# A two-layer hybrid encoder trunk on one core: the probability-times-value products of both attentions with high and low parts side by side in one matmul

## What is computed

```python
def hybrid_layer(x, w_in, a_group_w, a_scale, b_sinks, c_rel_bias, w_out, ln_gain, ln_bias):
    h = jnp.einsum('bsd,de->bse', x, w_in)
    a_v, a_gate, b_q, b_k, b_v, b_gate, c_q, c_k, c_v, c_gate = jnp.split(h, _split_points(), axis=-1)
    a_out = pool_mixer(a_v, a_group_w, a_scale) * jax.nn.silu(a_gate)
    b_out = swa_sink_attention(b_q, b_k, b_v, b_sinks) * jax.nn.silu(b_gate)
    c_out = chunk_relbias_attention(c_q, c_k, c_v, c_rel_bias) * jax.nn.silu(c_gate)
    mix = jnp.concatenate([a_out, b_out, c_out], axis=-1)
    y = jnp.einsum('bse,ed->bsd', mix, w_out)
    return _layer_norm(DEEPNORM_ALPHA * x + y, ln_gain, ln_bias)
# in both attentions
    p = jax.nn.softmax(s, axis=-1)            # B: with a sink column beside the keys
    o = jnp.einsum('bnhgqk,bnkhd->bnqhgd', p.astype(vb.dtype), vb)
```

## Time and profile before

| | us |
|---|---|
| median of 3 runs | 2956.86 (2956.52 to 2957.44) |
| the profiled execution, whole | 2955.86 |
| its span in the trace | 2954.1 |
| its mean granted TensorE clock | 0.998 |

### The profile page before, as it was taken

How to read it: one execution, slowest core, us unless ns; L and a number is a source line. 1 busy time by engine, 2 the same in 40 slices (tenths; PEclk the granted TensorE clock), 3 DMA queues, 4 the chain that set the end, 5 groups by cost and what they waited for, 6 DMA issues and landing times.

```text
span 2954.1 us, 46399 instructions
## 1 busy us (share of the span) xinstructions
PE 2923.3 (99%) x14272; PEld 2452.7 (83%) x14272; DVE 1408.8 (48%) x2546; ACT 1196.9 (41%) x2539; POOL 1252.6 (42%) x926
## 2 busy tenths in 40 slices
PE   8999999999999999999999999999999999999998
PEld 7888888888888888888888888888888888888886
DVE  5444555422666655531155555553126666555324
ACT  4443454422444445542244444553224444454421
POOL 4444444444344434444444444443443444344442
PEclk9999999999999999999999999999999999999999
DMA  6343332454344422335554442224553444233342
GB/s 195 118 122 119 87 83 76 131 174 161 117 143 139 138 82 76 83 115 156 151 165 143 146 146 86 80 81 135 168 172 95 146 139 138 79 82 82 125 150 107
DMA packets 189147, 364.13 MB, mean 123 GB/s; under 512 B 18913, under 2 KB 27137, under 8 KB 185345
## 3 DMA queue, kind: packets, MB, share of 16 engines
q1 hardware_dynamic: 185264, 347.25, 38.7%
q10 hardware_dynamic: 3792, 15.73, 1.3%
HBM read 320.94 MB, written 45.11 MB: 124 GB/s over the span
## 4 chain that ended last, share of the span: by engine, by line
PE 95%; issue 3%; DVE 2%; ACT 0%; POOL 0%; ACTq 0%; DVEq 0%; POOLq 0%
PE acc L523 64%; PE sc L523 17%; PE pv L523 11%; PE sc L583 2%; PE sc L629 1%; ACT mixl L861 0%; DVE nmax L1289 0%; DVE sc L1287 0%; PE acc L553 0%; PE pv L547 0%; PE sc L547 0%; DVE mixl L1248 0%; POOL wl L1206 0%; DVE prob L1296 0%; PE sc L559 0%
## 5 line engine op out<-in xcount | busy, mean ns | idle before, releaser
L1206 POOL TENSOR_TENSOR wl<-raw,wh 128x512 fp32r<-128x512 f32 x920 | 1251.9, 1366 | 1657.9 <-ACT wh L861 1621.1
L523 PE MATMUL acc<-xh,wh 128*128 128x512 f32 x2624 | 1037.8, 396 | 11.1 <-DVE xl L1237 7.9
L523 PE MATMUL acc<-xh,wl 128*128 128x512 f32 x2624 | 1024.5, 390 | 0.0
L523 PE MATMUL acc<-xl,wh 128*128 128x512 f32 x2624 | 1023.6, 390 | 0.0
L861 ACT ACTIVATE wh<-raw 128x512 fp32r<-128x512 f32 x920 | 569.1, 629 | 981.3 <-PE acc L523 608.4
L523 PEld LDWEIGHTS acc<-xh,wh 128*128 128x128 f32 x2624 | 493.7, 188 | 109.8 <-issue 10.0
L523 PEld LDWEIGHTS acc<-xh,wl 128*128 128x128 f32 x2624 | 493.1, 188 | 106.0
L523 PEld LDWEIGHTS acc<-xl,wh 128*128 128x128 f32 x2624 | 494.1, 188 | 95.3
L523 PE MATMUL sc<-wh,mixh 128*128 128x512 f32 x496 | 193.4, 390 | 0.1
L523 PE MATMUL sc<-wh,mixl 128*128 128x512 f32 x496 | 193.1, 389 | 0.0
L523 PE MATMUL sc<-wl,mixh 128*128 128x512 f32 x496 | 192.9, 389 | 0.0
(11 more groups left out here) (188 smaller groups left out, 3742.1 us busy)
## 6 DMA issues: line engine op xcount, KB each, us to landing
raw<-in_wall SPq DMA_DIRECT2D x920, 256.0 KB, 2.7
res_scratch<-res ACTq DMA_DIRECT2D x12, 1024.0 KB, 3.9
res<-res_scratch SPq DMA_DIRECT2D x12, 1024.0 KB, 5.0
res<-in_x SPq DMA_DIRECT2D x8, 1024.0 KB, 5.4
x_scratch<-res SPq DMA_DIRECT2D x8, 1024.0 KB, 4.7
prob<-x_scratch SPq DMA_DIRECT2D x32, 256.0 KB, 3.3
res<-x_scratch SPq DMA_DIRECT2D x8, 1024.0 KB, 5.2
hist_scratch<-mixh SPq DMA_DIRECT2D x8, 768.0 KB, 4.5
```

Source lines behind the costliest of these rows:

```text
L523: return nc.tensor.matmul(o, lhsT, rhs, start=start, stop=stop)
L1206: nc.gpsimd.tensor_tensor(wl[:, s, :], raw[:, s, :], wh[:, s, :].bitcast(F32), ALU.subtract).then_inc(w_lo, 1)
```

## The change

**C.** The values are now stored per head: `cv[h]` has the head's high part in 64 columns and its low part in the other 64, as `bv` has them. `pt` holds high and low probabilities side by side (`pt[:, block, head, part, query]`). `c_attend` runs, for each head and block, one matmul of 256 columns (128 queries, high and low): two matmuls for a block in place of three. The result of a group has four parts, one of which (low by low) was not computed before. ScalarE copies the lower 64 rows out (`c_low_rows`, between the two exponentials of the next group), VectorE adds them and then the two halves of the columns (`c_add`), into `c_att`. Each group has a bank of its own (the third takes the first one's again, the fourth one of `sc[0]`). `attention_product` becomes one operation.

**B.** `b_attend` takes both parts of a chunk in one matmul of 256 columns. A tile now fills two double banks, `pv` and `sc[g]`; ScalarE makes four copies in place of two, VectorE four adds of 64x512 and four of 64x256 in place of four of 64x256. `b_fold` counts twice for a tile.

**Order.** PE runs the first quarter of units 20 and 22 ahead of the transposes of groups 1 and 2. A's product goes behind the normalising of group 3. The tanh of a gate goes to the gate's own buffer. ScalarE's splits in the output projection stand one or two places earlier against the input's copies and the store of `res`.

```diff
-        pth = sb("pth", [P, 5, 2, P], F32R)
-        ptl = sb("ptl", [P, 5, 2, P], F32R)
+        pt = sb("pt", [P, 5, 2, 2, P], F32R)
+        pth, ptl = (pt[:, :, :, n, :] for n in range(2))
...
-        cv_h, cv_l = (m[:, MIX_B + 2:MIX_B + 4, :].rearrange("p a (b n) -> p (a b) n", n=P) for m in (mixh, mixl))
+        cv = [m[:, MIX_B + 2:MIX_B + 4, :].rearrange("p a (b n) -> p (a b) n", n=P) for m in (mixh, mixl)]
...
+        c_out = [pv[:, 0:512], pv[:, 512:1024], pv[:, 0:512], sc[0][:, 0:512]]
+        b_out = [[pv, sc[0]], [pv, sc[1]]]
...
             def c_attend(it, p, j):
-                if j == 0:
-                    pe.wait_ge(prod_ok, p * 2 + (MIXES * it + 2))
+                if j < 3:
+                    pe.wait_ge(c_fold, p * 4 + (4 * C_PAIRS * it + j + 1))
                 pe.wait_ge(ct_lo, p * 8 + (8 * C_PAIRS * it + 2 * j + 2 + 2))
                 v0 = 0 if half(it) else 4 - j
-                for v in range(v0, 5):
-                    *_, last = attend(outputs(j), (cv_h, cv_l), j + v, v, slice(0, P), v == v0, v == 4)
+                for h in range(2):
+                    for v in range(v0, 5):
+                        last = mm(c_out[j][:, 2 * P * h:2 * P * (h + 1)], cv[h][:, j + v, :],
+                                  pt[:, v, h, :, :].rearrange("p l q -> p (l q)"), v == v0, v == 4)
...
             def b_scores(it, v, g):
+                pe.wait_ge(b_fold, v * 2 + (2 * B_TILES * it + 1))
...
             def b_attend(it, v, g):
-                pe.wait_ge(b_fold, v + (B_TILES * it + 1))
+                pe.wait_ge(b_fold, v * 2 + (2 * B_TILES * it + 2))
                 for u in range(2):
                     pe.wait_ge(bt_lo, v * 2 + (2 * B_TILES * it + u + 1 + 4))
                     for c in range(4):
-                        n = 4 * u + c
-                        o = pv[:, P * n:P * (n + 1)]
-                        mm(o, bv[:, n, g, :], b_pth[:, u, c, :], True, False)
-                        last = mm(o, bv[:, n, g, :], b_ptl[:, u, c, :], False, True)
-                last.then_inc(b_pv, 1)
+                        last = mm(b_out[g][u][:, 2 * P * c:2 * P * (c + 1)], bv[:, 4 * u + c, g, :],
+                                  b_pt[:, u, c, :, :].rearrange("p l k -> p (l k)"), True, True)
+                    last.then_inc(b_pv, 1)
...
                     quarter(19, 0)
+                    quarter(20, 1, part=range(0, 1))
                     c_transpose(it, p, 1)
-                    quarter(20, 1)
+                    quarter(20, 1, part=range(1, 4))
...
                     nc.scalar.activation(prob[:, h, c0:C_KEYS], sc[h][:, at:at + C_KEYS - c0], ACT.Exp,
                                          bias=nmax[:, h, 0:1], accum_out=psums[:, h, 0:1]).then_inc(cs_exp, 1)
+                    if h == 0 and j:
+                        c_low_rows(it, p, j - 1)
...
+            def c_low_rows(it, p, j):
+                act.wait_ge(c_pv, p * 4 + (4 * C_PAIRS * it + j + 1))
+                act.wait_ge(c_fold, p * 4 + (4 * C_PAIRS * it + j + 1))
+                copy(c_low[ROWS[j % 2], :], c_out[j][HD:P, :]).then_inc(c_low_ok, 1)
...
+            def b_low_rows(it, v, g):
                 for u in range(2):
-                    last = copy(b_low[u], b_out[HD:P, 4 * u:4 * u + 4, :, :])
-                last.then_inc(b_low_ok, 1)
+                    act.wait_ge(b_pv, v * 2 + (2 * B_TILES * it + u + 1))
+                    act.wait_ge(b_fold, v * 2 + (2 * B_TILES * it + u + 2))
+                    for n, rows in enumerate(ROWS):
+                        last = copy(b_low(v, u)[rows, :], b_out[g][u][HD:P, 512 * n:512 * (n + 1)])
+                    last.then_inc(b_low_ok, 1)
...
+            def c_add(it, p, j):
+                dv.wait_ge(c_low_ok, p * 4 + (4 * C_PAIRS * it + j + 1))
+                low = c_low[ROWS[j % 2], :]
+                V_(V.tensor_tensor(low, c_out[j][0:HD, :], low, ALU.add))
+                sums_ = low.rearrange("p (h l q) -> p h l q", h=2, l=2)
                 for h in range(2):
+                    last = V.tensor_tensor(c_att[ROWS[h], P * j:P * (j + 1)], sums_[:, h, 0, :], sums_[:, h, 1, :], ALU.add)
+                last.then_inc(c_fold, 1)
...
                     c_lo(it, p, 2)
-                    dv.wait_ge(a_full, p + (pc + 1))
-                    V.scalar_tensor_tensor(tmp[:], acc[0][:, :], scale1[:], gate[:], ALU.mult, ALU.mult).then_inc(prod_ok, 1)
-                    mix_lo(p * 2 + (nb + 1), p + MIX_A)
+                    c_add(it, p, 0)
                     c_max(it, p, 3)
                     c_normalise(it, p, 3)
+                    dv.wait_ge(a_full, p + (pc + 1))
+                    V.scalar_tensor_tensor(tmp[:], acc[0][:, :], scale1[:], gates[0][:], ALU.mult, ALU.mult).then_inc(prod_ok, 1)
                     c_lo(it, p, 3)
+                    c_add(it, p, 1)
```

More of the change, by code:

```diff
@@ L277, in build @@
         c_pv = sem("c_pv")
+        c_low_ok = sem("c_low_ok")
+        c_fold = sem("c_fold")
         bs_full = sem("bs_full")
@@ L346, in unit, with b_low @@
             return r + it * U_STEP
+        def b_low(v, u):
+            if u == 0:
+                return av[:, 0:HALF]
+            return (fold_end if isinstance(v, int) and v >= B_TILES - 2 else fold_mid)[:]
         def probs(v):
@@ L689, in _ @@
                     quarter(21, 1)
+                    quarter(22, 1, part=range(0, 1))
                     c_transpose(it, p, 2)
@@ L697, in _ @@
                     mm(acc[0][:, :], gwl, ya_h, False, True).then_inc(a_full, 1)
-                    quarter(22, 1)
+                    quarter(22, 1, part=range(1, 4))
                     c_scores(it, p, 3)
@@ L1017, in _ @@
                     act.wait_ge(vn_full, p + ((C_PAIRS + 1) * it + 1))
-                    copy(cv_h[:, 4:8, :], acc[1][:, :].rearrange("p (b c) -> p b c", c=P)).then_inc(vh_ok, 1)
+                    for h in range(2):
+                        last = copy(cv[h][:, 4:8, 0:HD], acc[1][:, :].rearrange("p (b c) -> p b c", c=P)[:, :, ROWS[h]])
+                    last.then_inc(vh_ok, 1)
                     slot(10)
@@ L1149, in _ @@
                 gate_slot(5)
-                b_low_rows(it, last - 1)
+                b_low_rows(it, last - 1, 0)
                 gate_slot(6)
@@ L1154, in _ @@
                 used(it, O0 - 1)
-                act.wait_ge(gate_ok, MIXES * (it + 1))
+                split(it, O0, 0)
                 tanh_gate(1)
-                b_low_rows(it, last)
+                b_low_rows(it, last, 1)
+                split(it, O0 + 1, 1)
                 for n in range(2):
@@ L1177, in _ @@
                             act.dma_start(res_d[ds(n, 1)].rearrange("o p t n -> (o p) t n"), res[:]).then_inc(res_out, 16)
-            for u in range(RING_END - AHEAD):
+            for u in range(2, RING_END - AHEAD):
                 split(STEPS - 1, O0 + u, u % RING)
@@ L1227, in _ @@
             dv.sem_inc(ct_lo, 2)
+            dv.sem_inc(c_fold, 2)
             dv.sem_inc(bt_lo, 4)
-            dv.sem_inc(b_fold, 1)
+            dv.sem_inc(b_fold, 3)
             dv.sem_inc(prod_ok, 2)
@@ L1448, in _ @@
                     dv.wait_ge(vh_ok, p + ((C_PAIRS + 1) * it + 1))
-                    lo(cv_l[:, 4:8, :], acc[1][:, :].rearrange("p (b c) -> p b c", c=P), cv_h[:, 4:8, :])\
-                        .then_inc(v_ok, 1)
+                    for h in range(2):
+                        last = lo(cv[h][:, 4:8, HD:P], acc[1][:, :].rearrange("p (b c) -> p b c", c=P)[:, :, ROWS[h]],
+                                  cv[h][:, 4:8, 0:HD])
+                    last.then_inc(v_ok, 1)
                     dv.wait_ge(bias_in, p * 16 + (16 * pc + 16))
@@ L1562, in _ @@
                 b_lo(it, i, 0)
-                b_add(it, i, 0)
+                b_add(it, i, 0, (0,))
                 b_lo(it, i + 1, 1)
+                b_add(it, i, 0, (1,))
                 gate_of(i + 1, 1)
```

108 lines of the change are left out of this document (52 added, 56 removed).

## The result

The changed kernel takes 2917.2 us (median of four runs, 2914.5 to 2918.7) against 2956.8 us on the same chip: ratio 0.9865, 95% interval 0.9848 to 0.9882, 39.6 us less. The forecast was 2909.8 us. The time lies inside the range given, but 7.4 us above the forecast, and that difference has a structure worth reading.

What follows compares the result with a forecast made beforehand. PE, busy 99% of the span, was taken as the bound. Gross gain 28.8 + 26.6 = 55.4 us, less waits of 3.4, 3.0, 0.4 and 1.5, gave 47.1 us: 2908.8, plus 1.0 for the median, 2909.8 us; range 2901 to 2919.

Steps and rivals of the forecast that it cites:

- C's matmuls: C attends: two groups of 240 matmuls in place of three, 0.12 us each, saving 28.8 us.
- B's attends: B: 8 matmuls of 256 columns replace 16 of 128, next matmul 0.05 us sooner; 0.83 us a tile, 26.6 us.
- price by the row: B's narrow matmuls taken at the profile's 0.109 us, not the skill page's gap formula, which would save about 1 us.
- Group 3: C pairs: shortened attend leaves transposes and unit 24 waiting, 3.4 us in second halves and 3.0 us in first.
- Scores of group 2: C, second halves: cover behind group 2's transposes thins, 0.05 us of waiting, eight times, 0.4 us.
- B inside the loop: B loop: rotation moves 0.4 or 1.4 us, low part still 0.9 to 1.9 us ahead of second attend; costs nothing.
- The end of B: Steps 1 and 2: transposes of the next input wait for the last fold, 1.5 us for both.
- S + 6.55: C, second half: predicted start of unit 24, counted from S, the start of group 3's scores, after waiting for A's product.
- The first rival, no waits: Whole kernel: predicted delays overstated, all 55.4 us of gross gain stays, 2901.5 us; chance 0.14.
- The second, C gives back: C: only group 3's attends keep their gain, 20.2 us lost in place of 6.4, 2923.6 us; chance 0.09.
- The third: B gains nothing because 256 columns cost twice 128; 26.6 us fall away, 2936.4 us; chance 0.03.
- the fourth, slower: B loop: `b_add` delays the rotation so each round's second attend waits; 2969.8 us if 5 us beyond; chance 0.02.

Runs made afterwards that it cites:

- c_third: Changed kernel with each C attend issuing head 0's matmuls twice, so three groups of 256 columns as before the change: 2939.1 us, +22.5 us.
- b_narrow: Changed kernel with each B attend's 8 matmuls of 256 columns issued as 16 of 128, copies and adds kept: 2940.7 us, +24.1 us.
- g3_cover: Changed kernel with the last quarter of unit 22 (three matmuls, 0.68 us) issued behind group 3's scores instead of ahead: 2909.7 us, -6.9 us.

## Why the prediction was right, and where it was not

The working is compared with the starts in the two profiled executions, whose spans are 41.4 us apart; the forecast had 47.1.

- **C's matmuls, 28.8 us.** Measured 28.8, by the trace and again by `c_third`. Right.
- **B's attends, 0.78 + 0.05 us for each of 32, 26.6 us.** Measured 26.5 for the matmuls themselves (`b_narrow`, 0.79 and 0.05), 0.5 less in the changed kernel, where the `pt` wait stands ahead of four attends. Right, and with it the decision to price by the row.
- **Group 3, 3.4 + 3.0 us.** Measured 0.44 and 0.40 us in sixteen pairs, 6.7 us, with 0.3 us more in unit 24. Right in place, cause and size. Within it two small errors cancel: A's product ends at S + 6.44 where S + 6.49 was computed, and unit 24 starts 0.14 us behind it, not 0.06. The prediction expected to see these waits in the list; they are in the distances only. `g3_cover` confirms the reason given, an attend shortened with no quarter put in for it.
- **Scores of group 2, 0.4 us.** Measured 0.2. The wait on `c_fold` costs nothing, as said. A transpose's wait on `prob` grew by 0.3 us once.
- **B inside the loop, nothing.** Right: the low part starts at 395.57, its first half ends at 396.26, and the second attend starts at 398.56. By the prediction's own count, from that first half, 2.3 us are left where 0.9 to 1.9 were computed. In part that is luck: the rotation starts 0.6 us later against the attend (6.68 us, before 6.05), but its first operation, which took 1.26 us in the kernel before, takes 0.69 here.
- **The end of B, 1.5 us.** For the last fold 0.9 us a step were measured, 1.9 us for both, with 0.4 us back in step 0: right in place. But two terms are missing here. The `pt` wait costs 3.0 us and another 0.5 us in the attends behind it (the 0.5 of the second item), and the last step's gate 1.4 us.
- **The clock.** The median fell by 1.8 us less than the profiled execution. The text added the 1.0 us between median and profile of the kernel before; after the change that distance is 2.7 us. Falls of the clock at the start of B are the likely reason, but it is not shown: of the executions without a trace only the span and the mean granted clock to three digits are known, 0.998 in all three against 0.999 in the profiled one. That points the right way, and a single fall changes this mean by less than the last digit.

The sum then, with 7.0 for group 3 and unit 24, 0.5 for group 2 and the transpose, 3.5 for the `pt` wait, 1.5 for the last fold and 1.4 for the gate: 55.4 - 7.0 - 0.5 - 3.5 - 1.5 - 1.4 = 41.5 us, and 0.6 us of noise at the start, 40.9 against 41.4.

The step of the working that failed is the accounting of moves. The prediction priced each new operation and each new wait, but of ScalarE's `mix_hi`, moved behind the second tanh in the B loop, it said nothing. Its rule was right (behind a moved step, everything queued on it moves), and it was applied to C's product, where it gave S + 6.55 against 6.58, but not here. The diff of ScalarE's list has the line, and one look at who waits for `mixh` (VectorE's low part of that product, ahead of its gate) points at the 1.2 us. The split put ahead of the last tanh was counted for the last fold, but not for the gate that PE waits for in the last step. That the time still fell into the range is in part luck: its upper end doubled the waits that were named (8.3 us), and the waits came to 13.9 us because unnamed ones were added to them. The first rival, no waits, is out (13.9 us of them). The second, C gives back, is as near by its time (2923.6 against the measured 2917.2 us) as the forecast, and out by its mechanism: of its 20.2 us of waits in C the trace has 7.5, all but 0.5 of them at group 3. The third is out by `b_narrow`, and the fourth, slower, by the time.

## What to carry to other kernels

Price a matmul by the distance of starts at its own width, in its own data type: if two narrow ones cost twice a wide one, sharing a stationary side by side halves them. When a shorter stream has a dependent step behind it, move as much independent work ahead of that step as the stream lost; here 0.68 us, moved past one set of scores sixteen times, gave back 6 us. And list every instruction that a diff moves, per engine, with who waits for it, before the operations that it adds: the added work, 192 us on VectorE, cost little where nothing else moved, and two moved steps cost 5 us.

## What was not expected of the hardware

- Float32r matmuls, each with a new weight load, start 0.109 us apart at 128 columns (`b_narrow`) and 0.119 us at 256 (the changed kernel), so that the narrow form wastes nearly half; at 512 columns they are 0.227 us apart.
- A GpSimd subtraction of 1.29 us that starts just before a 0.69 us operation of VectorE on two SBUF inputs lengthens it to 1.7 to 1.8 us, and 128x4 operations from 0.15 to 1.28 us. Whether it hits is a question of phase: in a chain shifted by 1.2 us two normalisings and a 128x4 operation came under it.
- A wait of 1.0 us ahead of narrow matmuls was followed by a fall to the lower clock in 5 of 40 places, and the unit behind took 1.5 to 1.6 us longer each time; behind 4.3 us of waiting it came 4 times of 4, at 2.6 to 3.2 us each. So a wait can cost more than its length.
